# A transformer block with expert routing and row fetches, one core: the second half's attention is moved into the stage of the row fetches, its projections into the first half's tail

## The chip, the cores and the metric

The kernel runs on one core of one Trainium2 chip. The metric is the device time in microseconds of one execution. A core has the engines TensorE (PE, with its weight loads as PEld), VectorE (DVE), ScalarE (ACT), GpSimd (POOL) and SyncE (SP), each working through its own list of instructions in order, and 16 DMA engines. SP issues the weight loads, POOL issues indirect row fetches.

## The reference

All of it is float32, 256 tokens of width 1024. A first block (attention with a window, a convolution, a feed-forward of 16 experts) is followed by a second block, and only the second block matters here:

```
h = modulate(rmsnorm(x)); q, k, v, z, gl = split(h @ w_in)      # 7168 columns
q, k = rope(q), rope(k); k, v = concat(context, own)
for each of 8 heads: a = softmax(q1 k1) - lam * softmax(q2 k2); o = a @ v
y_attn = rmsnorm(o) @ w_branch_attn
y_sgu  = spatial_gating(gelu(z)) @ w_branch_sgu                  # per chunk of 128 tokens
x = x + gt1 * rmsnorm((sigmoid(ga) * y_attn + sigmoid(gs) * y_sgu) @ w_out)
# peer: 8 heads, each picks 16 of 16384 rows for each token
q = rmsnorm(modulate(rmsnorm(x)) @ w_query)
eidx, gate = two-stage top-16 of q @ sub_keys
out = sum_k gelu(h . u_tab[eidx_k]) * gate_k * v_tab[eidx_k]
return x + gt2 * rmsnorm(out)
```

## The kernel before

The 256 tokens are two halves of 128 (index `a`, 0 or 1). The second block, called the mixer here, follows one list of stages, `ORDER`, which `mixer_order` writes out; every engine walks the list and does its part of each stage, in order. The stages:

- `kq`, `vals`, `z`, `ga`, `gs`, `bs`, `ba`, `op` with `(n, a)` are "token groups": 16 matmuls (8 products, each as 2 instructions in the records) of one half against one 2 MB slab of weights (`tokens`, L379). `z` is the input of the spatial gating, `ga` and `gs` the gates, `bs` and `ba` the two branch products, `op` the output product. `zmix` (L689) mixes the tokens, `zturn` transposes its result.
- Attention has 16 units `ix` (half `a`, head `h`): `sc` (scores, L708), `exp` (DVE maxima L1199 to L1201, ACT exponentials L1629), `cmb` (DVE L1206 to L1213, with a scaled copy on ACT between, L1637), `trn` (transposes, L717), `av` (values, L728), `ao` (ACT).
- The tail of a half: `hn1`, `hn2`, `ht` (norm over the heads and transposes), `ba`, `bae`, `yt`, `op`, `ope`, `up1`, `up2`, `fn1`, `fn2`, `ft` (norms, residual, transposes L367). `gain1` and `gain2` spread a gain over the partitions (L737).
- The row stage: `take(a)` reserves four of the eight PSUM banks as accumulators, `qm(h, a)` (L771) and `qs` (L780) are the queries of one head (32 matmuls, slab `wq` of two heads), `back` turns the tokens back, `rt0` to `rt5` are the routing of one unit (DVE L1304 to L1379; the row numbers `ei` are ready after L1359). `row(ix, k)` is one fetch of 128 rows of 8 KB (1 MB, POOL L1739) and its dot product on DVE (L1368). `act` makes the weights on ACT (L1695, L1701), `v` multiplies two rows on PE (L813, 32 matmuls), which frees their two buffers. `leave(a)` (L825 on PE) folds the accumulators, applies a gain and a norm, and stores the half.

Order before. After `kq` and `vals`, ten steps handle units 0 to 7, each step followed by two token groups of a list `fill` of 20 (both halves of z, ga, gs, bs). Then comes the tail of half 0, and between its steps stand groups of the attention of units 8 to 15 (list `second`), two at a time. Then `take`, the queries of heads 0 to 3, nine more groups of `second`, `rt1` to `rt5` of unit 0, and the 256 rows. In the row stage one entry of the list `late` goes in at every third row: the queries of heads 4 to 7 of half 0, the tail of half 1, the queries of half 1. Routing stages stand at every row in unit 0 and at every odd row afterwards.

Weights: SP loads slabs into a ring of slots, [2, 3, 4, 5] in the mixer, [2, 3] once the row stage begins; a load waits until the slot's last user is done. A slab is loaded once for both halves in `z`, `ga`, `gs`, `bs`. Rows: eight buffers at first, four in the attention's scratch space (free after `av` of unit 15) and four in slots 4 and 5 (free after `op` of half 0), fixed in `row_places`; four more (slots 2 and 3) from the routing of unit 8 on.

Of the kernel before, what the change touches and what calls it, by code (L numbers as in the profile page):

```python
# [121 lines left out]
def build(nc, D, out):  # L122
    from contextlib import ExitStack
    ctx = ExitStack()
    with ctx:
# [71 lines left out]
        U, VV, SGT, GA = ar(o + 8192, 2, 1024), ar(o + 10240, 2, 1024), ar(o + 10240, 8, 256), ar(o + 12288, 2, 1024)  # L197
        RAW, RT, TMPG = ar(o + 14336, 2, 512), ar(o + 15360, 2, 512), ar(o + 14336, 2, 1024)
        PP, TT, AA, ATT = ar(o + 16384, 2, 2, 512), ar(o + 18432, 512), ar(o + 18944, 2, 512), ar(o + 19968, 2, 512)
        DM, OT, YT = ar(o + 20992, 16, 8), ar(o + 21120, 8, 128), ar(o + 22144, 8, 128)  # L200
        DG, G1, G2, OO, Y2 = ar(o + 10240, 8, 128), ar(o + 11264, 1024), ar(W0, 1024), XN, U
# [8 lines left out]
        RQ, DI, SG2 = ar(Q1 + 464, 2, 16), ar(Q1 + 496, 8, 2, 32), ar(o + 5120, 2, 16, 32)  # L210
# [14 lines left out]
        def mixer_order():  # L225
            todo = [("norm_turn", 0), ("kq", "k", 0, 0), ("norm_turn", 1), ("kq", "k", 0, 1), ("rope", "k", 0, 0)]
            held = ("rope", "k", 0, 1)
            for x, n in (("k", 1), ("q", 0), ("q", 1)):
                for a in range(2):
# [7 lines left out]
            def filler():  # L237
                while fill:
                    todo.append(fill.pop(0))
                    if todo[-1][0] in ("z", "ga", "gs", "bs"):  # L240
                        return

            for s in range(10):
# [6 lines left out]
                filler()  # L250
                if 1 <= s <= 8:
                    todo.append(("trn", s - 1))
                filler()
                if s >= 2:
                    todo += [("av", s - 2), ("ao", s - 2)]
            assert not fill
            second = []
            for s in range(8, 19):
                second.append([("sc", s)] * (s < 16) + [("trn", s - 2)] * (10 <= s < 18) + [("av", s - 3)] * (s >= 11))
                second.append([("cmb", s - 1)] * (9 <= s < 17) + [("exp", s)] * (s < 16) + [("ao", s - 3)] * (s >= 11))  # L260
# [34 lines left out]
            late = queries(2, 0) + queries(3, 0) + [h[0], h[1] + h[2]]  # L295
# [4 lines left out]
            for x in q[2:] + [[("back", 0)]] + queries(1, 0):  # L300
                todo += x
            queue(9)
            todo += [(f"rt{s}", 0) for s in range(1, 6)]
            routes = []
            for n in range(257):
# [9 lines left out]
                if n % 3 == 0 and late:  # L315
                    todo += late.pop(0)
# [6 lines left out]
            assert not late and not routes and not second  # L323
# [7 lines left out]
        ROWS = {}  # L331

        def row_places():
            def slots(i):
                return [NARENA + i * SLOT + x for x in range(0, 2 * SLOT, 2048)]

            bufs, n = [o + 16384, o + 18432, o + 2048, W0 + 2048] + slots(4), 0
            free = {k: ("mm", "av", 15) if i < 4 else ("used", "w_op", (i - 4) // 2, 0) for i, k in enumerate(bufs)}
            for stage, *x in ORDER:
                if (stage, *x) == ("rt0", 8):  # L340
                    new = slots(2)
                    free.update({k: ("used", "wq", 2 + i // 2, 1) for i, k in enumerate(new)})
                    bufs = bufs[:n] + new + bufs[n:]
                if stage == "row":
                    k = bufs[n]
                    n = (n + 1) % len(bufs)
                    ROWS[(*x,)] = k, free[k]
                    free[k] = ("mm", "row", x[0], x[1] // 2)

# [4 lines left out]
        def tensor(pe, w):  # L354
# [304 lines left out]
            def kq(x, n, a):  # L659
                tokens(("raw", x, n, a), ("w_in2", 2 + n if x == "k" else n), HT, a, h2m[a][:1], a == 1, h2m[a][1:])  # L660
# [10 lines left out]
            def vals(n, a):  # L671
                tokens(("vx", n, a), ("w_in2", 4 + n), HT, a, h2m[a], a == 1)

            def z(n, a):
                tokens(("z", n, a), ("w_in2", 6 + n), HT, a, h2m[a], a == 1)

            def ga(n, a):
                tokens(("gab", n, a), ("w_in2", 10 + n), HT, a, h2m[a], a == 1)

            def gs(n, a):  # L680
                tokens(("gsb", n, a), ("w_in2", 12 + n), HT, a, h2m[a], a == 1)
# [11 lines left out]
            def zturn():  # L693
                for a in range(2):
                    turn("copied", "sg", U[:, a, :], False, a, ("zmix", a, 1))

            def bs(n, a):
                tokens(("bs", n, a), ("w_bs", n), SGT, a, [("copied", "sg", 1, 1)], a == 1)
# [32 lines left out]
            def row_of(tag, *after):  # L731
                for q in range(2):
# [3 lines left out]
                    for j in range(4):  # L736
                        x = pe.matmul(PS[:, b, j * 128:(j + 1) * 128], ones, DG[:, 4 * q + j, :], start=True, stop=True)  # L737
# [5 lines left out]
            def ba(n, a):  # L743
                tokens(("ba", n, a), ("w_ba", n, a), OT, 0, [("scaled", "ot", a, 1)], True)
# [4 lines left out]
            def op(n, a):  # L749
                tokens(("y2sq", n, a), ("w_op", n, a), YT, 0, [("copied", "yt", a, 1)], True)  # L750
# [66 lines left out]
            def leave(a):  # L817
# [4 lines left out]
                for g in range(4):  # L822
                    w.wait_ge("part", a, g)
                    for m, (b, _) in enumerate(at):
                        x = pe.matmul(PS[32 * g:32 * g + 32, b, :], fold[:, m, :], PART[:, g, :], start=True, stop=True, skip_group_check=True)  # L825
                x.then_inc(*w.hit("mm", "leave", a, also=[("mm", "leave2", a)]))
# [11 lines left out]
        def vector(v, w):  # L838
# [376 lines left out]
            def row_of(tag, dst, col):  # L1215
                if tag == "g1":
                    w.wait_ge("mm", "bs", 1, 1)
# [6 lines left out]
                for j in range(8):  # L1224
                    i = v.tensor_scalar(DG[:, j, :], ident, col[:, j:j + 1], None, MULT)
# [19 lines left out]
            def heads_turn(a):  # L1245
                w.wait_step()
                w.wait_ge("gs", 1, 1)
                scaled("ot", OT, a, sub8, None)

            def bae(n, a):  # L1250
# [6 lines left out]
                w.wait_ge("bs", 1, 1)  # L1257
                v.tensor_tensor(y, y, g, ADD).then_inc(*w.hit("yy", n, a))

            def ope(n, a):  # L1260
                w.wait_ge("mm", "y2sq", n, a)
                w.wait_ge("row", "g1", 1)
                w.wait_ge("mm", "copied", "sg", 1, 1)
                v.tensor_tensor(Y2[:, a, n * 512:(n + 1) * 512], PS[:, banks.at("y2sq", n, a), :], G1[:, n * 512:(n + 1) * 512],
# [10 lines left out]
            def up2(a):  # L1275
                w.wait_ge("rstd", ("y2", a))
                w.wait_ge("y2", 1, a)
                v.scalar_tensor_tensor(X[:, a, :], Y2[:, a, :], ss5[:, a:a + 1], X[:, a, :], MULT, ADD).then_inc(*w.hit("x5", a))
# [91 lines left out]
            def rt5(ix):  # L1370
# [5 lines left out]
                w.wait_step()  # L1376
                if ix > 1:
# [4 lines left out]
            def leave(a):  # L1382
# [4 lines left out]
                for m in range(2):  # L1387
                    b = banks.at("leave", a, m)
                    w.wait_ge("sumsq", "out", a, m)
                    v.tensor_tensor(OUTS[a][:, m * 512:(m + 1) * 512], PS[:, b, :], G2[:, m * 512:(m + 1) * 512], MULT).then_inc(  # L1390
                        *w.hit("leave", a, m))
                w.step(v.tensor_tensor(SMX[:, a, 2:3], SMX[:, a, 2:3], SMX[:, a, 3:4], ADD))
                w.wait_step()
                rstd1(("out", a), SMX[:, a, 2:3], SMX[:, a, 2:3], 1024, 1e-6)
                rstd2(("out", a), SMX[:, a, 2:3])
                w.wait_ge("rstd", ("out", a))
                w.wait_ge("leave", a, 1)
                v.scalar_tensor_tensor(OUTS[a], OUTS[a], SMX[:, a, 2:3], X[:, a, :], MULT, ADD).then_inc(*w.hit("out", a))
# [12 lines left out]
        def scalar(act, w):  # L1411
# [197 lines left out]
            def zturn():  # L1609
                w.wait_ge("mm", "zmix", 1, 1)  # L1610
# [354 lines left out]
```

## Time and profile before

| what | value |
|---|---|
| median of 3 runs | 2239.13 us (2238.88 to 2240.02) |
| the profiled execution, its time | 2237.47 us |
| its span | 2235.7 us |
| PE busy | 1508.2 us (67%) |
| DVE busy | 753.6 us (34%) |
| ACT busy | 423.6 us (19%) |
| POOL busy | 297.8 us (13%) |
| read from HBM | 794.62 MB, 356 GB/s over the span |

The span is the profiled part of the execution; 1.8 us of its time lie around it. Busy shares are means over stages that differ: the first block runs up to about 1150 us, the mixer's dense part to about 1520 us, the row stage from there to the end. A clock of 1.00 is TensorE's full 2.4 GHz, 0.50 is 1.2 GHz.

### The profile page before, as it was taken

The numbers are of one execution on the slowest core, as the hardware profiler recorded it, in microseconds if no ns is written. First come the engines' busy times: TensorE is split into PE (matmuls) and PEld (weight loads), VectorE is DVE, ScalarE is ACT, GpSimd is POOL, SyncE is SP. The second block draws the span as 40 slices with busy tenths as digits, with TensorE's granted clock in tenths as the row PEclk, the third lists the DMA queues.
The fourth block names the chain that finished last, engine by engine and source line by source line (L and its number), as shares of the span: only waits on it lengthen the run. The fifth ranks groups of instructions, "written<-read, shape, count | busy, mean of one in ns | idle before, by whom it ended". The sixth has DMA issues, their size and how long they took to land.

```text
span 2235.7 us, 24542 instructions
## 1 busy us (share of the span) xinstructions
PE 1508.2 (67%) x10272; PEld 627.9 (28%) x10272; DVE 753.6 (34%) x1890; ACT 423.6 (19%) x983; POOL 297.8 (13%) x265
## 2 busy tenths in 40 slices
PE   8898756777766665665669999876655644444443
PEld 7555311332211111111124455454323421101010
DVE  5822101000000000000022141345657676776774
ACT  1321100000000000000011253243232332322221
POOL 0000000000000000000000000003333445444341
PEclk9988988988887878778779999987777865655555
DMA  9639999999999999999974332409999999999996
GB/s 382 236 152 423 427 426 427 426 427 427 428 426 427 427 427 427 427 427 426 428 319 170 135 139 84 188 18 367 420 419 377 420 416 415 412 420 420 419 419 270
DMA packets 74430, 797.46 MB, mean 357 GB/s; under 512 B 8304, under 2 KB 8432, under 8 KB 9424
## 3 DMA queue, kind: packets, MB, share of 16 engines
q1 hardware_dynamic: 37264, 527.25, 56.5%
q0 software_dynamic: 36864, 268.45, 29.1%
q8 instruction: 81, 1.33, 0.2%
q14 instruction: 29, 0.24, 0.0%
q10 hardware_dynamic: 192, 0.20, 0.0%
HBM read 794.62 MB, written 1.05 MB: 356 GB/s over the span
## 4 chain that ended last, share of the span: by engine, by line
DMA 46%; PE 32%; DVE 11%; POOL 4%; ACT 4%; issue 3%; another core or an unknown queue 0%; ACTq 0%; POOLq 0%; DVEq 0%
DMA AR<-in_w_down 18%; DMA AR<-in_w_up 15%; DMA AR<-in_peer_uv,AR 13%; PE PS L379 13%; POOL AR L1739 4%; DVE AR L1368 3%; PE PS L607 3%; PE PS L628 2%; PE PS L771 2%; PE PS L390 2%; PE PS L813 2%; PE PS L494 1%; DVE AR L890 1%; DVE AR L892 1%; PE PS L640 1%
## 5 line engine op out<-in xcount | busy, mean ns | idle before, releaser
L1739 POOL DMA_INDIRECT AR<-in_peer_uv,AR x256 | 296.0, 1156 | 1733.1 <-PE PS L728 1354.0
L813 PE MATMUL PS<-AR 32*32 32x512 f32 x4096 | 242.0, 921 | 328.5 <-ACT AR L1701 320.0
L607 PE MATMUL PS<-AR 128*32 128x512 f32 x2048 | 305.4, 734 | 181.0 <-DMA AR<-in_w_up 127.8
L1368 DVE CUSTOM_DVE_ANT_0 AR<-AR 128x1024 f32<-128x1024 f32 x256 | 309.7, 1222 | 166.3 <-DMA AR<-in_peer_uv,AR 153.1
L379 PE MATMUL PS<-AR 128*128 128x512 f32 x736 | 332.7, 607 | 2.4 <-DVE AR L865 1.9
L628 PE MATMUL PS<-AR 128*32 128x512 f32 x1024 | 173.3, 812 | 106.0 <-DMA AR<-in_w_down 99.2
L1064 DVE TENSOR_TENSOR AR<-AR,PS 128x512 f32<-128x512 f32 x16 | 11.0, 687 | 593.0 <-PE PS L607 593.0
L379 PEld LDWEIGHTS PS<-AR 128*128 128x128 f32 x736 | 140.2, 195 | 174.9 <-issue 174.6
L813 PEld LDWEIGHTS PS<-AR 32*32 32x32 f32 x4096 | 46.2, 127 | 479.9 <-ACT AR L1701 443.0
L607 PEld LDWEIGHTS PS<-AR 128*32 128x32 f32 x2048 | 63.9, 123 | 411.8 <-DMA AR<-in_w_up 204.3
L1078 DVE COPY AR<-PS 128x512 f32<-128x512 f32 x16 | 11.1, 691 | 284.7 <-PE PS L628 284.7
L628 PEld LDWEIGHTS PS<-AR 128*32 128x32 f32 x1024 | 33.5, 130 | 225.9 <-DMA AR<-in_w_down 149.8
L1522 ACT ACTIVATE AR<-PS 128x512 f32<-128x512 f32 x16 | 9.6, 597 | 398.4 <-PE PS L607 398.4
L390 PE MATMUL PS<-AR 128*128 128x256 f32 x384 | 83.4, 379 | 0.9 <-DVE AR L860 0.9
L640 PE MATMUL PS<-AR 128*128 128x512 f32 x128 | 68.4, 683 | 14.3 <-DVE AR L1078 13.5
L390 PEld LDWEIGHTS PS<-AR 128*128 128x128 f32 x384 | 72.9, 190 | 11.8 <-issue 2.0
L1695 ACT ACTIVATE AR<-AR 128x2 f32<-128x2 f32 x128 | 25.7, 201 | 249.0 <-DVE AR L1368 232.0
L771 PE MATMUL PS<-AR 128*128 128x128 f32 x512 | 70.7, 304 | 1.1 <-ACT PS L1651 1.1
L771 PEld LDWEIGHTS PS<-AR 128*128 128x128 f32 x512 | 68.2, 218 | 10.4 <-issue 10.4
L1701 ACT ACTIVATE AR<-AR 128x32 f32<-128x32 f32 x256 | 68.4, 314 | 9.2 <-ACT AR L1695 0.4
L1531 ACT COPY AR<-PS 128x512 f32<-128x512 f32 x16 | 9.4, 585 | 309.4 <-PE PS L617 309.4
L640 PEld LDWEIGHTS PS<-AR 128*128 128x128 f32 x128 | 26.7, 220 | 65.9 <-issue 65.9
(271 smaller groups left out, 1247.3 us busy)
## 6 DMA issues: line engine op xcount, KB each, us to landing
AR<-in_w_gate SPq DMA_DIRECT2D x64, 2048.0 KB, 26.1
AR<-in_w_up SPq DMA_DIRECT2D x64, 2048.0 KB, 24.7
AR<-in_w_down SPq DMA_DIRECT2D x64, 2048.0 KB, 26.0
AR<-in_w_in SPq DMA_DIRECT2D x23, 2048.0 KB, 8.7
AR<-in_w_ada SPq DMA_DIRECT2D x12, 2048.0 KB, 10.2
AR<-in_peer_w_query SPq DMA_DIRECT2D x8, 2048.0 KB
AR<-in_w_out SPq DMA_DIRECT2D x6, 2048.0 KB, 11.4
AR<-in_w_branch_attn SPq DMA_DIRECT2D x4, 2048.0 KB
```

Source lines behind the costliest of these rows:

```text
L379: i = pe.matmul(PS[:, b, :], src[:, j, a * 128:(a + 1) * 128], IN[key][:, j, :], start=(j == 0), stop=(j == 7))
L390: i = pe.matmul(PS[:, b, q * 256:(q + 1) * 256], IN[key][:, j, (e + q) * 128:(e + q + 1) * 128], src[:, j, :], start=(j == 0), stop=(j == 7))
L494: x = pe.matmul(PS[:, b, :], MT[:, 4 * q + j, a * 128:(a + 1) * 128], IN[key][:, j, n * 512:(n + 1) * 512], start=(j == 0), stop=(j == 3))
L607: x = pe.matmul(PS[32 * q:32 * q + 32, bk, :], XS[:, j, e * 32:(e + 1) * 32], IN[key][:, jj, q * 512:(q + 1) * 512], start=(j == 0), stop= ...
L628: x = pe.matmul(PS[32 * g:32 * g + 32, b, :], HDT[:, s, fq * 32:(fq + 1) * 32], IN[key][:, s, dc * 512:(dc + 1) * 512], start=(fq == 0 and ...
L640: x = pe.matmul(PS[:, y, :], GE[:, r, dc, a * 128:(a + 1) * 128], EO[:, r, :], start=(e == 0), stop=(e == 15), skip_group_check=True)
L771: x = pe.matmul(PS[:, b, q * 128:(q + 1) * 128], IN[key][:, j, (2 * r + q) * 128:(2 * r + q + 1) * 128], HT[:, j, a * 128:(a + 1) * 128], ...
L813: x = pe.matmul(PS[c:c + 32, ACC[a][g], :], DI[t, p, r, :], AR[t, off + 1024 + m * 512:off + 1536 + m * 512], start=(h == 0 and p == 0), s ...
L1368: v.tensor_tensor_reduce(rows, rows, HB[:, a, :], 1.0, 0.0, MULT, ADD, DOT[:, ix, k:k + 1]).then_inc(*w.hit("dot", ix, k))
L1695: w.step(act.activation(two, DOT[:, ix, 2 * p:2 * p + 2], ACT.Gelu))
L1701: i = act.activation(DI[:, p, r, :], SG2[:, ix % 2, 2 * p + r, :], ACT.Copy, scale=two[:, r:r + 1])
L1739: pool.indirect_dma_start(out=AR[:, off:off + 2048], out_offset=None, in_=D["peer_uv_2"], in_offset=bass.IndirectOffsetOnAxis(ap=EI[:, ix, ...
```

## The change

- The list of token groups is split. `first` (12 groups) keeps `z` 2 and 3 of both halves and everything of half 0; it stands between the steps of units 0 to 7, one group a step (two in steps 0 and 8). `then` (10 groups with `zmix` and `zturn` of half 1, that is `z`, `ga`, `gs`, `bs` of half 1) stands between the steps of half 0's tail, and its last, `bs(1, 1)`, after `rt5` of unit 0.
- The attention of units 8 to 15 (22 list entries) moves to the head of `late`, and `late` is taken at every second row in place of every third. Five empty entries stand before half 1's `ba`.
- All queries of half 0 stand before the first row.
- Slabs `z` 0 and 1, `ga`, `gs`, `bs` are loaded once for each half. The slot ring is [5, 2, 3, 4].
- The first eight row buffers are the two halves of each slot of the ring, free once `wq` 0, 1, 2, 3 of half 0 are used. After `ao` of unit 15 the four buffers of the scratch space come in, and slots 5 and 2 leave for weights; `w_ba` of half 1 waits for the last rows in them. Slots 5 and 2 come back at the routing of unit 8.
- `SGT`, `OT`, `YT`, `DG`, `Y2` become one tile for each half, `SG2` and `G1` move, and a few waits follow them.
- `leave` takes its two column halves apart: matmuls, squares, the last product and the store go half by half, and for half 1 ACT runs a square root on a spare value before the last rows are done.

```diff
-            fill = [("z", 2, 0), ("z", 2, 1), ("z", 3, 0), ("z", 3, 1), ("zn1",), ("z", 0, 0), ("zn2",), ("z", 0, 1), ("zn3",), ("z", 1, 0),
-                    ("z", 1, 1), ("zmix", 0), ("ga", 0, 0), ("zmix", 1), ("ga", 0, 1), ("ga", 1, 0), ("zturn",), ("ga", 1, 1)]
-            fill += [(f, n, a) for f in ("gs", "bs") for n in range(2) for a in range(2)]
+            first = [("z", 2, 0), ("z", 2, 1), ("z", 3, 0), ("z", 3, 1), ("zn1",), ("z", 0, 0), ("zn2",), ("z", 1, 0), ("zn3",), ("ga", 0, 0),
+                     ("zmix", 0), ("ga", 1, 0), ("zturn", 0), ("gs", 0, 0), ("gs", 1, 0), ("bs", 0, 0), ("bs", 1, 0)]
+            then = [("z", 0, 1), ("z", 1, 1), ("zmix", 1), ("ga", 0, 1), ("zturn", 1), ("ga", 1, 1), ("gs", 0, 1), ("gs", 1, 1), ("bs", 0, 1),
+                    ("bs", 1, 1)]
...
-            steps = h[:2], h[2:] + [[("gain1",)]], b[0], b[1], y, p[0], p[1], u[:2], u[2:4], u[4:]
-            for group in steps:
+            for group in (h[:2], h[2:] + [[("gain1",)]], b[0] + b[1], y, p[0] + p[1], u[:2], u[2:4]):
                 for x in group:
                     todo += x
-                queue(2)
+                filler(then)
+            todo += u[4]
...
-            late = queries(2, 0) + queries(3, 0) + [h[0], h[1] + h[2]]
+            late = []
+            for s in range(8, 19):
+                late.append([("sc", s)] * (s < 16) + [("trn", s - 2)] * (10 <= s < 18) + [("av", s - 3)] * (s >= 11))
+                late.append([("cmb", s - 1)] * (9 <= s < 17) + [("exp", s)] * (s < 16) + [("ao", s - 3)] * (s >= 11))
+            late += [h[0], h[1] + h[2]] + [[]] * 5
...
-            for x in q[2:] + [[("back", 0)]] + queries(1, 0):
+            for x in q[2:] + [[("back", 0)]]:
                 todo += x
-            queue(9)
             todo += [(f"rt{s}", 0) for s in range(1, 6)]
+            filler(then)
+            for x in queries(1, 0) + queries(2, 0) + queries(3, 0):
+                todo += x
...
-                if n % 3 == 0 and late:
+                if n % 2 == 0 and late:
                     todo += late.pop(0)
...
+        RING = [5, 2, 3, 4]
+            halves = [[NARENA + i * SLOT, NARENA + i * SLOT + 2048] for i in RING]
+            free = {k: ("used", "wq", i, 0) for i in range(4) for k in halves[i]}
+            bufs, gone = sum(halves, []), []
             for stage, *x in ORDER:
-                if (stage, *x) == ("rt0", 8):
-                    new = slots(2)
-                    free.update({k: ("used", "wq", 2 + i // 2, 1) for i, k in enumerate(new)})
-                    bufs = bufs[:n] + new + bufs[n:]
+                if (stage, *x) == ("ao", 15):
+                    new = [o + 2048, W0 + 2048, o + 16384, o + 18432]
+                    free.update({k: ("mm", "av", 15) for k in new})
+                    bufs, gone = bufs + new, halves[0] + halves[1]
+                elif (stage, *x) == ("rt0", 8):
+                    free.update({k: ("used", "wq", 2 + i, 1) for i in range(2) for k in halves[i]})
+                    bufs = bufs + halves[0] + halves[1]
...
+                if key[0] == "w_ba" and key[2] == 1:
+                    for half in (0, 2048):
+                        w.wait_ge(*LATEST[place[slot] + half])
...
             def leave(a):
+                if a:
+                    w.wait_ge("out", 0, 1)
+                    act.activation(SMX[:, 0, 3:4], ones[:, 0:1], ACT.Sqrt)
...
-                v.scalar_tensor_tensor(OUTS[a], OUTS[a], SMX[:, a, 2:3], X[:, a, :], MULT, ADD).then_inc(*w.hit("out", a))
+                for m in range(2):
+                    d = OUTS[a][:, m * 512:(m + 1) * 512]
+                    w.wait_ge("leave", a, m)
+                    v.scalar_tensor_tensor(d, d, SMX[:, a, 2:3], X[:, a, m * 512:(m + 1) * 512], MULT, ADD).then_inc(*w.hit("out", a, m))
```

## Rows read from the trace of the kernel before

**Rows 1.** The page's chain that ended last, shares by engine.
```profile
DMA 46%; PE 32%; DVE 11%; POOL 4%; ACT 4%; issue 3%; another core or an unknown queue 0%; ACTq 0%; POOLq 0%; DVEq 0%
```

**Rows 2.** Windows: stretch, length, busy of each engine, clock, DMA share, GB/s.
```profile
1157.00:1521.00 364.00, 336.55 (x1199) 182.93 (x1200) 108.10 (x275) 122.13 (x254) 0.95 (x1) 0.95 0.33 125
1521.00:1848.00 327.00, 195.06 (x2284) 101.19 (x2282) 220.03 (x577) 103.39 (x269) 132.97 (x113) 0.74 1.00 411
```

**Rows 3.** DMA queues from 1521 to 2219 us: packets, MB, share.
```profile
q0 software_dynamic: 36864, 268.45, 93.1%
q1 hardware_dynamic: 1368, 18.22, 6.2%
```

**Rows 4.** Timeline of DVE, ACT and SP at the span's end: start, length.
```profile
2162.65 1.22 DVE L1368 CUSTOM_DVE_ANT_0 AR<-AR 128x1024 f32<-128x1024 f32 x1
2163.80 1.22 DVE L1368 CUSTOM_DVE_ANT_0 AR<-AR 128x1024 f32<-128x1024 f32 x1
...
2216.55 1.23 DVE L1368 CUSTOM_DVE_ANT_0 AR<-AR 128x1024 f32<-128x1024 f32 x1 [1.26 <-DMA AR<-in_peer_uv,AR]
2219.03 1.22 DVE L1368 CUSTOM_DVE_ANT_0 AR<-AR 128x1024 f32<-128x1024 f32 x1 [1.24 <-DMA AR<-in_peer_uv,AR]
...
2229.57 1.28 ACT L1415 ACT_TABLE_LOAD   x1
...
2231.30 1.29 DVE L1398 SCALAR_TENSOR_TENSOR AR<-AR 128x1024 f32<-128x1024 f32 x1
```

**Rows 5.** Timeline of PE, steps of units 0 to 7 with token groups.
```profile
1253.88 1.14 PE L708 MATMUL PS<-AR 64*128 64x256 f32 x8
...
1276.91 0.60 PE L717 MATMUL PS<-PK,AR 128*128 128x128 f32 x4
1277.35 7.03 PE L379 MATMUL PS<-AR 128*128 128x512 f32 x16
...
1327.22 1.95 PE L689 MATMUL PS<-AR,PK 128*128 128x128 f32 x16
```

**Rows 6.** Timeline of PE, half 0's tail and queries.
```profile
1416.29 1.05 PE L728 MATMUL PS<-AR 128*128 128x128 f32 x8
...
1425.54 3.76 PE L737 MATMUL PS<-AR,PK 128*128 128x128 f32 x16 [3.33 <-DVE AR L1225]
...
1494.23 5.41 PE L771 MATMUL PS<-AR 128*128 128x128 f32 x32 [1.06 <-ACT PS L1651]
...
1507.57 3.74 PE L771 MATMUL PS<-AR 128*128 128x128 f32 x32
...
1512.75 3.82 PE L771 MATMUL PS<-AR 128*128 128x128 f32 x32
```

**Rows 7.** Timeline of DVE: one unit of attention, routing (first, last), first row.
```profile
1431.48 0.75 DVE L1213 SCALAR_TENSOR_TENSOR AR<-AR 128x512 f32<-128x512 f32 x1 [0.79 <-ACT AR L1637]
1432.14 0.68 DVE L1199 TENSOR_REDUCE AR<-PS 128x1 f32<-128x512 f32 x1
...
1502.10 0.61 DVE L1304 TENSOR_SCALAR AR<-PS,AR 128x128 f32<-128x128 f32 x2
...
1512.06 0.17 DVE L1359 CAST AR<-AR 128x16 uint32<-128x16 f32 x1
...
1527.71 1.23 DVE L1368 CUSTOM_DVE_ANT_0 AR<-AR 128x1024 f32<-128x1024 f32 x1 [4.96 <-DMA AR<-in_peer_uv,AR]
```

**Rows 8.** Timeline of POOL: the first row fetch.
```profile
1520.05 1.08 POOL L1739 DMA_INDIRECT AR<-in_peer_uv,AR  x1 [1353.99 <-PE PS L728]
```

**Rows 9.** Line L1368 (dots of rows) from 1521 to 1848 us.
```profile
L1368 DVE CUSTOM_DVE_ANT_0 AR<-AR x109: 1202/1222/1265, 1527.7 to 1845.7; 128x1024 f32<-128x1024 f32 x109
```

**Rows 10.** Timeline of PE, two token groups in the row stage.
```profile
1602.45 9.29 PE L379 MATMUL PS<-AR 128*128 128x512 f32 x16
...
1612.74 7.13 PE L379 MATMUL PS<-AR 128*128 128x512 f32 x16
```

**Rows 11.** Windows of 10 us in the row stage, the emptiest (columns as rows 2).
```profile
1690.00:1700.00 10.00, 4.96 (x76) 2.13 (x74) 7.12 (x23) 5.29 (x13) 2.24 (x2) 0.78 0.59 220
```

More of the change, by code:

```diff
@@ L249, in mixer_order @@
                     todo.append(("exp", s))
-                filler()
+                filler(first)
                 if 1 <= s <= 8:
                     todo.append(("trn", s - 1))
-                filler()
+                if s in (0, 8):
+                    filler(first)
                 if s >= 2:
                     todo += [("av", s - 2), ("ao", s - 2)]
[L256 to L260, printed above, removed]
+            assert not first
             def tail(a):
@@ L691, in zmix, with zturn @@
                     x.then_inc(*w.hit("mm", "zmix", a, q))
-            def zturn():
-                for a in range(2):
-                    turn("copied", "sg", U[:, a, :], False, a, ("zmix", a, 1))
+            def zturn(a):
+                turn("copied", "sg", U[:, a, :], False, a, ("zmix", a, 1))
             def bs(n, a):
-                tokens(("bs", n, a), ("w_bs", n), SGT, a, [("copied", "sg", 1, 1)], a == 1)
+                tokens(("bs", n, a), ("w_bs", n, a), SGT[a], 0, [("copied", "sg", a, 1)], True)
             def att_scores(ix):
@@ L1607, in zn1, with zturn @@
                     act.activation(Y[:, a, :], VV[:, a, :], ACT.Square, accum_out=smv[:, 4 + a:5 + a]).then_inc(*w.hit("sumsq", "zv", a))
-            def zturn():
-                w.wait_ge("mm", "zmix", 1, 1)
-                for a in range(2):
-                    copied("sg", SGT[:, :, a * 128:(a + 1) * 128], a)
+            def zturn(a):
+                w.wait_ge("mm", "zmix", a, 1)
+                copied("sg", SGT[a], a)
             def ga(n, a):
@@ L1823, in sync @@
                     load(NS + 3, ("rows",), D["rows"].partition_broadcast(128), 2, 1024)
-                elif stage == "bs" and x[1] == 0:
-                    square(("w_bs", x[0]), "w_branch_sgu_2", x[0])
-                elif stage == "gain1":
-                    turn[0] = 0
+                elif stage == "bs" and x != [1, 1]:
+                    square(("w_bs", *x), "w_branch_sgu_2", x[0])
                 elif stage == "take" and x[0] == 0:
-                    turn[0], ids[0] = 0, [2, 3]
+                    square(("w_bs", 1, 1), "w_branch_sgu_2", 1)
+                    assert turn[0] % 4 == 0
+                elif (stage, *x) == ("hn1", 1):
+                    turn[0], ids[0] = 0, RING[:2]
                 elif stage == "ba":
@@ L1837, in sync @@
                     a = x[0]
-                    w.wait_ge("out", a)
-                    sp.dma_start(out[a * 128:(a + 1) * 128, :], OUTS[a]).then_inc(*w.hit("stored", a, by=16))
-            w.wait_ge("stored", 1)
+                    for m in range(2):
+                        f = slice(m * 512, (m + 1) * 512)
+                        w.wait_ge("out", a, m)
+                        sp.dma_start(out[a * 128:(a + 1) * 128, f], OUTS[a][:, f]).then_inc(*w.hit("stored", a, m, by=16))
+            w.wait_ge("stored", 1, 1)
         for dry in (True, False):
```

102 lines of the change are left out of this document (54 added, 48 removed).

## The prediction

> **What bounds the kernel now.** I read the chain that ended last first: it lies on DMA for 46% and on PE for 32% [rows 1]. Windows tell where. From 1157 to 1521 us PE is busy for 336.6 of 364 us while DMA is busy for a third; from 1521 us on DMA is busy throughout and PE for 60% [rows 2]. So there are two stages: a dense one that PE's sum sets, and a row stage that the DMA traffic sets, from the first fetch on. Work that goes from the first under the second is free as long as it keeps the fetches fed. In the row stage 268.45 MB are rows and 18.22 MB the other traffic [rows 3]; where nothing disturbs it a row comes every 2.49 us (2216.55 to 2219.03) [rows 4]. A DVE dot costs 1.15 us when two follow each other [rows 4], so DVE has 1.34 us to spare for each row. The first dot starts at 1527.7 us and the 109th at 1845.7 us [rows 9]; 108 rows of 2.49 us and eight slabs of 5 us (2.1 MB at 420 GB/s) are 309 us, so 9 us of DMA time are lost in this half, some 4 of them near 1695 us, in half 1's tail [rows 11].
>
> **Before the rows.** The dense stage is costed as a sum on PE. A token group takes 7.0 us (7.03 less the overlap with its neighbour), `zmix` 1.9 for a half, `zturn` 0.9 for a half (8 matmuls where `zmix` has 16 in 1.95) [rows 5]. A unit of attention costs PE 1.06 + 0.44 + 0.98 = 2.5 us (L708, L717, L728, start to start) [rows 5, 6]. The first scores start at 1253.9 us. The ten steps keep 12 groups (83.5 us), 8 units (19.8), one `zmix` and one `zturn` (2.8): 106 us. Each step is now 9.5 us instead of 16.4; a unit's work on DVE is 3.5 us (cmb 0.75, maxima 2 x 0.68, small ones, 0.8 of waiting for ACT's copy) [rows 7], so it fits, and I add 2 us for stalls (0 to 6). The last `av` then ends at 1362 us; before it does at 1417.3 [rows 6].
>
> The tail of half 0 now has whole token groups between its steps. On PE: ten groups before `ft` (z 2, ba 2, ga 2, op 2, gs 2: 70), one more (bs, 7), `zmix`, `zturn`, `yt` (3.7), `ht` with the stall and `gain1` (1.0 + 3.3 + 3.8 [rows 6]) = 89 us, then 4.6 us from the start of `ft` to the first query (transposes, four DVE products of 0.7). The norms of the tail hide under the groups: each is a pass or two over a half and a root, 1.3 us each [rows 4], and a group lasts 7. Queries start at 1455.4 us (before 1494.2). From that start to `ei` it was 17.9 us (1512.1) [rows 6, 7], of which 1.7 us are a slow clock (5.41 against 3.74 us for one query) [rows 6]. The first row can be issued at 1472 us, 48 us earlier than at 1520.05 [rows 8].
>
> But it isn't worth 48 us. The fetches of rows 2 and 3, 4 and 5, 6 and 7 wait for queries 3, 5 and 7, and `v` of rows 0 and 1, which frees the next buffers, stands in PE's list behind all of them. PE: query 0 and rt0 5.7 us, query 1 and `back` 6.0, `bs(1, 1)` 7.0, six queries at 5.2 (1507.57 to 1512.75 [rows 6]) 31.2; PE reaches the rows at 1505.3 us, and queries 3, 5, 7 end at 1483, 1493.4 and 1503.8. ACT's and DVE's lists have the same barrier: the root in `rt0` of unit 1 stands behind the last query. From there DVE sets the pace: dots 1 to 7 (8.1), routing of unit 1 (11.5: 10.1 from 1502.1 to 1512.2 [rows 7], and an estimate of 1.4 for rt0 and rt5), two units' maxima and one `cmb` (5.2), 25.3 us in all, to 1530.6. With `act` 0.7, `v` 2.0 and the issue 0.3, rows 14 and 15 are issued at 1533.7; a fetch lands 5.4 us after its issue (1520.05 to 1527.7, less 2.2 us for a rest of a slab that is still under way: 18.22 MB less eight slabs and the store of 0.5 is 0.9 MB) [rows 3, 7, 8]. Row 14 lands at 1539.1; at 2.49 us a row that is as if row 0 had landed at 1504.2, against 1527.7: **-23.5 us**.
>
> **Under the rows.** Eight units over 44 rows (109.6 us of DMA). DVE's sum: 44 dots 50.6, three routings 34.5, eight units 28 = 113 us. It falls behind by 4 us in 16 rows and is some 11 us late at row 44. A ring of eight buffers (19.9 us) forgives 9 us, so I take 3 us of loss; the bounds are 0 (waits overlap) and 10 (each step waits 1 us more). It doesn't come back, since DMA is the bound afterwards. The tail of half 1 goes at two rows a step (5.0 us, or 7.5 where a slab is loaded too) instead of three: four token groups of 7.1 to 9.3 us [rows 10] and eight `v` of 1.1 to 2.0 us stand against 16 rows (40 us) with some four slabs (20 us), 54 us of PE against 60 of DMA. But in the three steps of norms DVE waits 3 us for ACT's root each time, and each step is now 2.5 us shorter, 7.5 us together; before, such a place cost 4 us [rows 11]. I take 5 us of loss; the bounds are 0 and 12. The queries of half 1 fit (17 us of PE against 15 and two slabs in a cycle of three steps). DMA's bytes hardly change: slabs that are now loaded twice are loaded in the dense stage, where DMA is busy for a third [rows 2], 5 us of traffic in a group of 7 us, four slots ahead; the 0.9 MB fall away, already counted.
>
> The clock: in the dense stage 0.95 is granted, in the row stage 0.74 [rows 2], and a token group takes 9.29 us after a lull and 7.13 right behind another [rows 10]. The Trainium skill says in "TensorE: Matmul & The Clock Gate", section "What's actually happening", that the array runs at half rate by default and activity releases it; this trace agrees (0.95 against 0.74). By that rule, units moved to where PE is sparse cost 40 instead of 20 us of PE and the four groups 37 instead of 28, which PE's slack takes up.
>
> **The end.** `leave` of half 1: the 1.28 us table load before the root goes off the chain, and the last product of 1.29 us is split [rows 4]. About 0.4 us of the load are covered by DVE's work; the last piece ends 0.9 us earlier, its store is smaller: **-1.3 us** (bounds -0.5 and -2.5).
>
> **Sum.** -23.5 + 3 + 5 - 1.3 = -16.8 us, on the profiled execution's own 2237.5 us: 2220.7. That execution is 1.7 us below the median of the runs, so 2222 us.
>
> **Rivals.**
> - *The rows stay fed from the queries on.* If DVE gets ahead in the first eight rows (waits of ACT and PE overlap more than I count) and the tail loses nothing new, row 6 issued at 1503.8 lands at 1509.2, as if row 0 had landed at 1494.3: -33.4 - 1.3 = -35, 2204 us. For it: DVE is busy for 220 of 327 us there [rows 2]. Against: 25 us of DVE work stand in its first eight rows.
> - *The whole 48 us come.* Needs rows 2 to 7 not to wait for the queries; the buffers exclude it. About 2190, nearly no chance.
> - *The other side: the steps at every second row.* In the first 104 rows DVE has 120 us of dots, 75 of routing, 28 of attention and some 39 of tail, gains and norms, 262 us, against 299 us of DMA (104 x 2.49 and eight slabs). With the ring's 9 us, what DVE waits for PE and ACT in these 52 steps beyond 46 us (0.9 us a step) is lost. I have put 8 us of loss; at 1.4 us of waiting a step 25 us are lost and the gain is nothing, at 1.7 us a step it ends at 2255 us. For it: DVE waits 0.8 us for ACT in each unit [rows 7] and PE holds `v` back for 7 to 9 us at a token group. Against: DVE idles for a third of this half now [rows 2].
> - *Weights late in the dense stage.* Ten more slabs; against it the ring is four deep, 28 us of work. Each late slab would cost up to 5 us; it takes three to be seen.
>
> **How the numbers follow.** Under 0.2% (4.5 us) this kernel's measurement can't tell a change from none. My forecast with its own bounds (2212 to 2234) has a chance of 0.5, fed from the start (below 2212) 0.28, a result within 4.5 us of before 0.1 and slower 0.12, nearly all of both by the steps at every second row. The range leaves out a tenth on each side: 2200 to 2240. Faster 0.78, same 0.10, slower 0.12.
>
> **What would show it.** The profile after should have the last `av` of unit 7 near 1362 us, the first query near 1455, the first fetch near 1472, rows 2, 4 and 6 issued near 1483, 1493 and 1504, then dense fetches from about 1534. DMA's share should be 1.00 from there with short holes in the attention's last rows and in half 1's tail, and the last dot starts near 2203. I am wrong if holes of more than 25 us together stand in the first 104 rows, if PE waits for slabs before the rows, or if DVE isn't what paces the first eight rows.

## The result, and the profile after

The changed kernel takes 2251.92 us (median of 4 runs, 2251.43 to 2254.99) against 2239.01 us for the kernel before beside it: ratio 1.0061, interval 1.0043 to 1.0078. It is slower; the forecast was 17 us faster. The profiled execution took 2251.69 us with a span of 2249.9, 14.2 us longer than before.

The page's slices already show two different halves of the answer: DMA works much more in the dense stage, and has holes where it used to be full. Windows of the kernel after, columns as in [rows 2]:

```profile
1154.00:1465.00 311.00, 298.80 (x944) 152.12 (x945) 87.30 (x220) 94.37 (x178) 0.00 (x0) 0.97 0.53 197
1465.00:1540.00 75.00, 45.07 (x446) 31.42 (x444) 35.89 (x97) 30.41 (x66) 20.85 (x18) 0.77 0.70 258
1540.00:1860.00 320.00, 187.03 (x2044) 99.32 (x2028) 201.21 (x536) 121.20 (x293) 107.27 (x93) 0.71 0.89 355
```

The dense stage is over 56 us earlier than in [rows 2]. In exchange the stage behind it, which ran at 1.00 of DMA before (the second window of [rows 2]), runs at 0.89, and in the mean of its 320 us no engine is full: DVE 63%, PE 58%, ACT 38%.

The dense part went as the forecast says. Timeline of PE after (L737 is `av`, L746 `gain1`, L780 the first query), to be laid beside [rows 6]:

```profile
1355.97 1.05 PE L737 MATMUL PS<-AR 128*128 128x128 f32 x8
...
1367.34 2.59 PE L746 MATMUL PS<-AR,PK 128*128 128x128 f32 x16 [2.58 <-DVE AR L1235]
...
1446.80 5.44 PE L780 MATMUL PS<-AR 128*128 128x128 f32 x32 [2.64 <-DVE AR L874]
```

and of POOL, which answers to [rows 8]:

```profile
1465.17 1.08 POOL L1758 DMA_INDIRECT AR<-in_peer_uv,AR  x1 [1302.00 <-DVE AR L1370]
...
1476.36 0.94 POOL L1758 DMA_INDIRECT AR<-in_peer_uv,AR  x1 [8.86 <-PE PS L780]
...
1486.87 0.94 POOL L1758 DMA_INDIRECT AR<-in_peer_uv,AR  x1 [8.34 <-PE PS L780]
...
1497.38 0.94 POOL L1758 DMA_INDIRECT AR<-in_peer_uv,AR  x1 [8.33 <-PE PS L780]
...
1512.43 1.87 POOL L1758 DMA_INDIRECT AR<-in_peer_uv,AR  x1 [5.30 <-PE PS L822]
...
1528.77 0.94 POOL L1758 DMA_INDIRECT AR<-in_peer_uv,AR  x1 [4.90 <-PE PS L822]
```

The first fetch is issued at 1465 us (before 1520), rows 2, 4 and 6 wait for queries 3, 5 and 7 (L780), and row 14 goes out at 1528.8 where 1533.7 was forecast. The gain is there at that point. The next table tells where it goes: the start of row n's dot product, in us, read from DVE's timeline of each kernel (one profiled execution of each; executions of one kernel differ by some us, so small differences of such stretches say little).

| row | before | after | after minus before |
|---|---|---|---|
| 0 | 1527.7 | 1471.0 | -56.7 |
| 8 | 1553.3 | 1524.4 | -28.9 |
| 48 | 1681.7 | 1646.6 | -35.1 |
| 72 | 1751.5 | 1742.2 | -9.3 |
| 112 | 1855.7 | 1872.8 | +17.1 |
| 255 | 2219.0 | 2234.9 | +15.9 |

Rows 8 to 112 need, by the prices of the prediction, 104 x 2.49 us and eight slabs of 5 us, 299 us of DMA. Before took 302.4, after takes 348.4: 3 us lost before, 49 after. The kernel before has issued six of its eight slabs by row 48 (at 1540.6 to 1649.7 us), the changed one none (its first at 1655.8), so -35.1 at row 48 hides that it is behind already: its 122.2 us for 40 rows are 22.6 more than their 99.6 of DMA, and the next 64 rows with eight slabs (199.4 us) lose 27 more. From row 112 on both run at the pace of DMA.

What such a hole is made of, in an attention entry. Timeline of the kernel after (L822 is `v`, L717 `sc`, L726 `trn`, L1659 ACT's copy of the transposes, L1698 the routing's exponential, L1711 and L1717 the weights of two rows):

```profile
1578.82 2.02 PE L822 MATMUL PS<-AR 32*32 32x512 f32 x32 [6.62 <-ACT AR L1717]
...
1580.78 2.08 PE L717 MATMUL PS<-AR 64*128 64x256 f32 x8
...
1582.78 1.09 PE L726 MATMUL PS<-PK,AR 128*128 128x128 f32 x4
...
1583.91 0.59 ACT L1659 COPY AR<-PS 128x512 f32<-128x512 f32 x1 [5.14 <-PE PS L726]
...
1584.52 1.28 ACT L1698 ACT_TABLE_LOAD   x1
...
1585.81 0.31 ACT L1698 ACTIVATE AR<-AR 128x16 f32<-128x16 f32 x1
...
1586.23 1.28 ACT L1711 ACT_TABLE_LOAD   x1
...
1587.53 0.20 ACT L1711 ACTIVATE AR<-AR 128x2 f32<-128x2 f32 x1
...
1587.76 0.53 ACT L1717 ACTIVATE AR<-AR 128x32 f32<-128x32 f32 x2
...
1588.35 2.02 PE L822 MATMUL PS<-AR 32*32 32x512 f32 x32 [3.58 <-ACT AR L1717]
```

One `v` follows another after 9.5 us, where two rows of DMA last 5.0. It is one of the three longest such rounds of rows 8 to 48, where a pair of rows takes 6.1 us in the mean. The 9.5 us are a chain with one link after another: `v` 2.0, `sc` 2.0, `trn` 1.1, ACT's copy 0.6, a table load 1.3, the exponential 0.4, another load 1.3, the weights 0.8. The dots of those two rows had ended at 1581.9; their weights wait in ACT's list until 1587.5, behind a copy that waits for PE, and PE had this `trn` behind the previous `v`. In the tail of half 1 the same list waits for DVE:

```profile
1739.94 2.02 PE L822 MATMUL PS<-AR 32*32 32x512 f32 x32 [5.68 <-ACT AR L1717]
...
1742.21 1.22 DVE L1379 CUSTOM_DVE_ANT_0 AR<-AR 128x1024 f32<-128x1024 f32 x1
...
1747.97 1.22 DVE L1379 CUSTOM_DVE_ANT_0 AR<-AR 128x1024 f32<-128x1024 f32 x1
...
1752.15 0.15 DVE L1371 TENSOR_SCALAR AR<-AR 128x1 f32<-128x1 f32 x1
...
1752.33 0.31 ACT L1698 ACTIVATE AR<-AR 128x16 f32<-128x16 f32 x1 [11.14 <-DVE AR L1371]
1752.75 1.28 ACT L1711 ACT_TABLE_LOAD   x1
...
1754.04 0.20 ACT L1711 ACTIVATE AR<-AR 128x2 f32<-128x2 f32 x1
...
1754.86 2.02 PE L822 MATMUL PS<-AR 32*32 32x512 f32 x32 [8.74 <-ACT AR L1717]
...
1757.80 0.95 POOL L1758 DMA_INDIRECT AR<-in_peer_uv,AR  x1 [12.32 <-PE PS L822]
```

The two dots are done at 1749.1. Their weights stand behind the routing's exponential, which waits until DVE has finished that unit's routing at 1752.2. ACT idles for 11 us, and POOL gets its next free buffer after 12.3 us. DMA's share is 0.53 in the window from 1750 to 1760 us. The order is not all of this hole: the dots themselves end only at 1749.1, since DVE does work of the tail between them and is busy for 8.5 and 9.7 of the 10 us from 1740 and from 1750 on. The order costs what lies between 1749.1 and 1754.0, when the weights start: 4.9 us. So DVE, at 63% in the mean, is full in just this place.

### The profile page after: what moved, and what is told of

Read it like the earlier page. It is cut to its first block, busy times and chain, and to the rows that moved or that the text cites. A ratio compares the mean times of both kernels' runs of the same rounds, so it can differ in the third digit from the quotient of the medians.

```text
span 2249.9 us, 24580 instructions
## 1 busy us (share of the span) xinstructions
PE 1503.2 (67%) x10272; PEld 625.4 (28%) x10272; DVE 751.3 (33%) x1892; ACT 445.1 (20%) x1000; POOL 295.2 (13%) x265
## 4 chain that ended last, share of the span: by engine, by line
DMA 43%; PE 34%; DVE 12%; ACT 6%; POOL 3%; issue 2%; ACTq 0%; POOLq 0%; DVEq 0%
DMA AR<-in_w_down 18%; DMA AR<-in_w_up 15%; PE PS L389 14%; DMA AR<-in_peer_uv,AR 10%; PE PS L780 3%; POOL AR L1758 3%; DVE AR L1379 3%; PE PS L822 3%; PE PS L617 2%; PE PS L638 2%; PE PS L400 2%; DVE AR L899 1%; PE PS L504 1%; DVE AR L901 1%; ACT L1711 1%
## 5 line engine op out<-in xcount | busy, mean ns | idle before, releaser
L822 PE MATMUL PS<-AR 32*32 32x512 f32 x4096 | 233.5, 945 | 363.4 <-ACT AR L1717 363.4
L1379 DVE CUSTOM_DVE_ANT_0 AR<-AR 128x1024 f32<-128x1024 f32 x256 | 308.2, 1221 | 126.7 <-DMA AR<-in_peer_uv,AR 126.7
L389 PEld LDWEIGHTS PS<-AR 128*128 128x128 f32 x736 | 140.4, 194 | 175.0 <-issue 174.3
L822 PEld LDWEIGHTS PS<-AR 32*32 32x32 f32 x4096 | 41.8, 127 | 508.9 <-ACT AR L1717 498.0
L400 PEld LDWEIGHTS PS<-AR 128*128 128x128 f32 x384 | 72.9, 190 | 12.0 <-issue 2.2
L1711 ACT ACTIVATE AR<-AR 128x2 f32<-128x2 f32 x128 | 25.8, 202 | 235.3 <-DVE AR L1379 234.6
L780 PE MATMUL PS<-AR 128*128 128x128 f32 x512 | 70.0, 302 | 2.6 <-DVE AR L874 2.6
L780 PEld LDWEIGHTS PS<-AR 128*128 128x128 f32 x512 | 67.5, 216 | 10.8 <-issue 10.8
L1717 ACT ACTIVATE AR<-AR 128x32 f32<-128x32 f32 x256 | 68.3, 314 | 9.3 <-ACT AR L1711 0.7
L1711 ACT ACT_TABLE_LOAD x41 | 52.6, 1283 | 0.7
```

Source lines behind the costliest of these rows:

```text
L389: i = pe.matmul(PS[:, b, :], src[:, j, a * 128:(a + 1) * 128], IN[key][:, j, :], start=(j == 0), stop=(j == 7))
L400: i = pe.matmul(PS[:, b, q * 256:(q + 1) * 256], IN[key][:, j, (e + q) * 128:(e + q + 1) * 128], src[:, j, :], start=(j == 0), stop=(j == 7))
L780: x = pe.matmul(PS[:, b, q * 128:(q + 1) * 128], IN[key][:, j, (2 * r + q) * 128:(2 * r + q + 1) * 128], HT[:, j, a * 128:(a + 1) * 128], ...
L822: x = pe.matmul(PS[c:c + 32, ACC[a][g], :], DI[t, p, r, :], AR[t, off + 1024 + m * 512:off + 1536 + m * 512], start=(h == 0 and p == 0), s ...
L1379: v.tensor_tensor_reduce(rows, rows, HB[:, a, :], 1.0, 0.0, MULT, ADD, DOT[:, ix, k:k + 1]).then_inc(*w.hit("dot", ix, k))
L1711: w.step(act.activation(two, DOT[:, ix, 2 * p:2 * p + 2], ACT.Gelu))
```

## The experiments

Theory "queue": the weights of two rows, which free their buffers through `v`, stand in ACT's list behind work that waits for PE or DVE, and that loop takes longer than the fetches of two rows. Against it: "sum" (DVE or PE has too much work at any spacing), "ring" (the eight buffers in slots that weights share), "tables" (ACT's table loads are the long part). Each kernel below was timed beside the kernel before on its own chip, so ratios are compared; 1.0061 is the changed kernel's. The intervals stand in brackets.

**Spacing.** In each kernel one condition is changed; the first two also have fewer empty entries.

```diff
 # att3_rest2
-            late += [h[0], h[1] + h[2]] + [[]] * 5
+            late += [h[0], h[1] + h[2]] + [[]] * 2
-                if n % 2 == 0 and late:
+                if (n % 3 == 0 if n < 66 else n % 2 == 0) and late:
 # att2_rest3
-            late += [h[0], h[1] + h[2]] + [[]] * 5
+            late += [h[0], h[1] + h[2]] + [[]] * 0
-                if n % 2 == 0 and late:
+                if (n % 2 == 0 if n < 44 else (n - 44) % 3 == 0) and late:
 # before_step2, in the kernel before
-                if n % 3 == 0 and late:
+                if n % 2 == 0 and late:
```

> Changed kernel with one edit: the 22 attention entries at every third row, the rest still at every second (two of the five empty entries kept so that it fits). Theory 'step' (each entry makes DVE, ACT and PE wait for one another inside two rows' time; some 28 us of fetch time are lost over rows 0 to 48 and some 27 over the tail and queries of half 1): the first loss falls to about 10 us, the second stays, so about 2235 us. Theory 'sum' (DVE has too much work whatever the spacing): no change, 2250 us or more. Theory 'ring' (eight buffers among slots that weights share are the cause): no change.

2232.56 us, ratio 0.9974 (0.9964 to 0.9984). The attention at every third row takes back 19 us. Rows 8 to 48 now take 109.9 us instead of 122.2, rows 48 to 112 213.9 instead of 226.2. Over rows 8 to 112 together that is 323.8 us instead of 348.4, while DVE is busy for 219 us of them (217 in the changed kernel), so "sum" falls. 5 us of this are given back in rows 112 to 128 (56.6 instead of 51.5), where the last two queries of half 1 now stand. The split between the two stretches says less, since 13 attention entries stand in rows 8 to 47 at this spacing and 18 in the changed kernel. The second loss shrank although six attention entries moved into it, which was not expected.

> Changed kernel with one edit: attention entries at every second row as now, the tail and queries of half 1 at every third, no empty entries. Theory 'step': the loss over rows 48 to 112 falls from 27 us to the 9 us that the kernel before shows in all this half, about 2234 us; the attention's loss stays. Theory 'sum': the same 2250. Theory 'ring': about 2250, and without the empty entries PE waits for slabs, 5 us more.

2258.1 us, ratio 1.0096 (1.0073 to 1.0118): a miss for all the theories as they stood. Two things cancel. PE's timeline shows long waits before its two `ba` groups, since the empty entries that gave their slabs time are gone (the first wait has no releaser in the profile; its slab was issued at 1657.9, 11.6 us ahead of the group):

```profile
1669.52 9.38 PE L389 MATMUL PS<-AR 128*128 128x512 f32 x16 [11.75 <-issue]
...
1689.00 9.88 PE L389 MATMUL PS<-AR 128*128 128x512 f32 x16 [9.04 <-DMA AR<-in_w_branch_attn]
```

Rows 48 to 72 take 107.7 us (95.6 in the changed kernel), rows 72 to 112 take 115.5 (130.6). So rows 72 to 112 gained 15 us, and the missing empty entries took 12. Not all of the 15 is won: at this spacing the last two queries of half 1 stand behind row 110, and rows 112 to 128 take 4 us more (55.5 for 51.5).

> The kernel before with one edit: its late entries at every second row instead of every third (nothing else of the change). Theory 'step': the denser steps alone cost it some 10 to 20 us, 2249 to 2259 us. Theories 'sum' and 'ring': work and buffers are the same, so 2239 us, within 4 us.

2250.09 us, ratio 1.0053 (1.0035 to 1.0071). With none of the change's moves, every second row alone costs the kernel before 11 us: rows 8 to 112 take 315.4 us instead of 302.4. The denser steps are a cost of their own.

**The attention back ahead of the rows.**

```diff
-            for x in queries(1, 0) + queries(2, 0) + queries(3, 0):
+            for x in units[:4]:
                 todo += x
+            for i, x in enumerate(queries(1, 0) + queries(2, 0) + queries(3, 0)):
+                todo += x
+                for y in units[4 + 2 * i:min(22, 4 + 2 * i + 2)]:
+                    todo += y
```

(`units` are the 22 attention entries, taken out of `late`.)

> Changed kernel with its attention of half 1 put back before the rows, between the queries of heads 2 to 7, where DVE idles for some 30 us; the rest as in the changed kernel (every second row, five empty entries). Eight units cost PE some 20 us there, so rows from the eighth on come about 20 us later; the 28 us of loss over rows 0 to 48 should go under theories 'step' and 'sum' alike: 2240 to 2246 us. Under 'ring' the loss stays and it is 20 us worse, 2270 us.

2261.32 us, ratio 1.0109 (1.009 to 1.0128): worse, and not for the ring. Row 8's dot starts at 1570.9 us, 46 us later than in the changed kernel where 20 were expected, since PE waits for ACT's exponentials between the queries. One of these places, on PE (L784 are the queries there):

```profile
1482.58 5.47 PE L784 MATMUL PS<-AR 128*128 128x128 f32 x32 [3.33 <-ACT AR L1649]
```

From row 8 to 112 it takes 310.1 us, 11 more than DMA needs, at the same two-row steps. That does not settle "ring", because the buffers are not the same: the exchange of buffers hangs on `ao` of unit 15, which now stands ahead of row 0, so that from row 8 on four of the eight lie in the scratch space, as in the kernel before. Against "ring" stand before_step2, which loses its 13 us without the changed ring, and the next edit, which leaves the ring as it is. Units of attention without token groups between them cost 46 us ahead of the rows and, if the whole difference is theirs, some 38 (49 less 11) under them.

**ACT's order.** In the row stage ACT's part of the transposes, the queries and the routing's exponential goes behind the next weights; nothing else moves. This is the edit to ACT's walk through the list:

```diff
             for stage, *x in ORDER:
-                if stage in mine:
+                rows = rows or stage == "row"
+                if rows and stage in ("trn", "qm", "rt4"):
+                    late.append((stage, x))
+                elif stage in mine:
                     mine[stage](*x)
+                if stage == "act":
+                    for name, y in late:
+                        mine[name](*y)
+                    late = []
```

> Changed kernel with ACT's own order edited in the row stage: its part of the transposes, of the queries and of the routing's exponential goes behind the next weights of rows instead of ahead of them. Theory 'queue' (the weights of two rows, which free their buffers through v, stand in ACT's list behind work that waits for PE or DVE; the loop dot, entry, weights, v, fetch then takes longer than two rows of DMA): at least 20 of the 45 us of extra loss go, about 2225 us. Theory 'engines too full' (DVE's or PE's sum): 2250 us, no change. Theory 'step' without the queue behind it (PE and DVE waits alone): 2245 to 2250 us.

2224.12 us, ratio 0.9935 (0.9919 to 0.9952): 28 us of the changed kernel's time gone by an order of instructions alone, with the same ring, spacing and work; between 1500 and 1860 us ACT loads a table 48 times instead of 50, so it is not fewer table loads. Rows 8 to 112 take 311.4 us instead of 348.4 (row 8 itself starts 7 us later, at 1531.2). Rows 48 to 112 take 197.9, their DMA time. Rows 8 to 48 take 113.5 instead of 122.2: 14 of the 22.6 us lost there stay. Windows of this kernel:

```profile
1465.00:1540.00 75.00, 46.17 (x423) 32.53 (x421) 34.37 (x100) 26.78 (x59) 17.61 (x17) 0.82 0.64 237
1540.00:1830.00 290.00, 181.24 (x2092) 95.83 (x2092) 203.81 (x539) 121.69 (x297) 110.97 (x96) 0.76 0.98 399
```

DVE's 204 us fit in 290 us (before the edit 201 in 320), and DMA is at 0.98. The list of waits from 1500 to 1860 us (engine and line, who for, us in all, times, longest) says which wait became which. After:

```profile
POOL AR L1758 <- PE PS L822: 221.7, 43, 12.3
...
DVE AR L856 <- ACT AR L1430: 64.1, 10, 28.1
ACT AR L1711 <- DVE AR L1379: 50.5, 10, 13.4
ACT AR L1686 <- PE PS L780: 46.5, 8, 8.0
ACT AR L1659 <- PE PS L726: 34.6, 8, 5.2
ACT AR L1698 <- DVE AR L1371: 29.8, 4, 11.1
```

and in act_first:

```profile
POOL AR L1768 <- PE PS L822: 182.7, 49, 12.6
...
ACT AR L1711 <- DVE AR L1379: 115.1, 34, 14.0
...
DVE AR L856 <- ACT AR L1430: 38.4, 11, 28.1
ACT AR L1686 <- PE PS L780: 27.1, 9, 5.2
```

ACT's weights now wait for their own dot products (L1379), 34 times instead of 10, and its waits for PE's transposes (L1659) are 10.6 us in all and those of the routing's exponential for DVE (L1698) 4.1. DVE gains too: its waits for a square root on ACT (L856) fall from 36.0 to 10.3 us, when the 28.1 us behind the barrier of queries are left out.

The three parts one by one, each with only its own stage in the tuple `("trn", "qm", "rt4")`:

> Changed kernel; of the edit of ACT's order only the routing's exponential is moved behind the next weights. The whole edit brought 28 us. ACT stood up to 11 us before this exponential once for each of seven units of half 0: if that is the main part, 13 to 18 us of the 28 come, 2237 us; if the queue behind PE (transposes, queries) is, under 8 us, 2246 us.

2241.51 us, ratio 1.0017 (1.0007 to 1.0027).

> Changed kernel; only ACT's part of the queries is moved behind the next weights. ACT waited 46 us for the eight queries of half 1: if these waits sit in the loop, 8 to 12 us of the 28 come, 2242 us; if DMA was fed anyway there, nothing, 2252 us.

2239.35 us, ratio 1.0002 (0.9992 to 1.0011).

> Changed kernel; only ACT's copy of the transposed weights of attention is moved behind the next weights. ACT waited 35 us for the eight transposes: if these waits sit in the loop, 5 to 10 us of the 28 come, 2244 us; if DVE's sum bounds the attention's rows, nothing, 2252 us.

2240.74 us, ratio 1.0009 (0.9998 to 1.0019).

Against 1.0061 these are 10, 13 and 12 us, 35 together where all three at once give 28: three of the same kind, none of them the main one. The queries' part works mostly in rows 88 to 112 (62.6 us instead of 74.6), the transposes' part mostly in rows 8 to 48 (113.4 instead of 122.2).

> The kernel before with the same edit of ACT's order. Its row stage has DMA at 1.00 nearly everywhere, so under any theory little is to be had: 'queue' gives 2234 to 2239 us (part of the 9 us lost in half 0), the others 2239 us.

2232.88 us, ratio 0.9964 (0.9952 to 0.9976), 8 us less, somewhat more than expected. The queue is in the kernel before as well; at three rows a step it costs it little.

> Changed kernel in which the rows' weights leave out the Gelu (a plain copy of the dot product in its place), so that ACT needs no table load before them. Theory 'tables' (two loads of 1.28 us for each unit, root or exponential, lengthen the loop): of 45 us of extra loss 15 to 25 go, about 2230 us. Theory 'queue' with waits for PE and DVE as the long part: 5 to 10 us go, about 2243 us.

2232.56 us, ratio 0.9964 (0.9952 to 0.9976), 22 us below the changed kernel, as "tables" had it. This kernel leaves out the Gelu, and between 1500 and 1860 us it loads a table 15 times instead of 50. So "tables" stands beside "queue" and does not fall. The two don't contradict each other: the loads are links of the same chain, and the chain gets shorter by any of its links. No kernel has both edits, so what they share is not known.

> Attention entries at every third row (2232.6 us alone) with the edit of ACT's order. Theory 'queue': the losses left there (10 us over rows 8 to 48, 15 over 48 to 112) halve, about 2220 us. If spacing and order cure the same thing in full, 2230 us; 'engines too full' 2233 us.

2211.96 us, ratio 0.9884 (0.9862 to 0.9906), the fastest kernel here: 26 us below the one before. Rows 8 to 112 take 308.3 us, 9 above DMA's time, and rows 8 to 48 of them 105.7, 6 above theirs.

**The barrier of queries.** Two conditions and a list: the queries of heads 6 and 7 leave the front and come first in `late`.

```diff
-            for x in queries(1, 0) + queries(2, 0) + queries(3, 0):
+            for x in queries(1, 0) + queries(2, 0):
-            late = []
+            late = queries(3, 0)
-                if (n % 3 == 0 if n < 66 else n % 2 == 0) and late:
+                if (n % 2 == 0 if n < 6 or n >= 72 else n % 3 == 0) and late:
```

> The kernel with attention at every third row and the edit of ACT's order (2212 us), in which the queries of heads 6 and 7 also go behind the first rows (entries at rows 0, 2 and 4). If the barrier of queries before the rows is what leaves DMA at 0.6 to 0.8 from 1480 to 1540 us, PE reaches the rows 10 us earlier and 5 to 9 us come: 2205 us. If DVE's routing in the first eight rows is, 2212 us.

2213.24 us, ratio 0.9891 (0.9873 to 0.9908): no gain over 0.9884. Row 8 starts at 1515.1 us instead of 1524.0, as expected of the barrier, and row 112 at 1818.6 instead of 1832.3, but at row 128 the two are level (1883.1 and 1884.5). The last 16 rows of the half take 64.5 us (52.2 in att3_act_first). The trace shows two reasons. The last `wq` slab of half 1 is issued at 1825.5 us, behind row 112 here and ahead of it there (1816.5), which only moves 5 us. The rest is a hole, with DMA's share at 0.39 from 1850 to 1860 us. The fetch of row 124 goes to slot 2, which is free only when slab `wq` 3 is used up, and the query that ends its use stands behind row 122 here and behind row 116 there. So POOL stands before this fetch for 10.5 us (4.0 in att3_act_first), with all later fetches behind it. This, too, is an item that waits at the head of an engine's list, this time POOL's.

## Why the prediction was wrong

- **The start of the rows** (-23.5 us) was right in its mechanism and 5 us too careful, by its own steps: 1356.8 us for the end of the last `av` (forecast 1362), 1446.8 for the first query (1455), 1465 for the first fetch (1472), 1528.8 for row 14 (1533.7). Half of the difference was there when the first scores started, at 1251.2 instead of 1253.9 us; most of the rest are the 2 us of stalls that I had added and that did not come. DVE did pace the first eight rows: it waited until 1500.4 us for the root behind the last query (forecast 1505.3) and ended dot 7 at 1524.5, 24.1 us later. The recorded parts of that stretch (8.1, 11.5 and 5.2) add up to 24.8 us, not 25.3. Row 8 is 28.9 us earlier than before.
- **Attention under the rows (+3 us, bounds 0 to 10) is the step that failed first.** It measured 22.6 us over rows 8 to 48. The step compared DVE's sum with DMA's time and gave the ring 9 us of forgiveness. (By its own sum, 113 us against 109.6, DVE would be 3.5 us late at row 44 and not 11.) But DVE's sum didn't set the pace: DVE was busy for 86.1 of the 122.2 us, less than the 99.6 that DMA needs. What was missing is the round from one `v` to the next, through three engines' lists, which a sum per engine can't see because none of the three is full in the mean. ACT alone waited 34.6 us there for PE's transposes (L1659), in eight places. How much of the 22.6 us is ACT's order is shown in part: act_first takes 9 away with the same work in the same rows. The other 14 stay at this spacing; with the attention at every third row as well (att3_act_first) it is 6. Which waits of PE and DVE make them up is open.
- **The tail at every second row (+5 us, bounds 0 to 12)** measured 27 us over rows 48 to 112, where the kernel before, with two slabs left, loses some 5. The step looked for DVE's waits for the roots of the norms, 3 us each; in the trace they are 0.7, 1.1 and 1.4 us. The long waits of this stretch were ACT's, for PE's queries (46.5 us in eight places) and for DVE's routing (17.9 in two), and behind ACT those of DVE for the root of a routing's start (9.2 us before 1776.9 and 10.4 before 1836.1). act_first takes all of these 27 us away, and before_step2 shows that the denser steps cost 13 us over rows 8 to 112 without the rest of the change.
- **The end** (-1.3 us): from the start of the last dot to the end of the span it was 16.7 us [rows 4] and is 15.0, so -1.7. The table load before the root is off the chain, at 2236.99, beside the last `v`:

```profile
2234.87 1.23 DVE L1379 CUSTOM_DVE_ANT_0 AR<-AR 128x1024 f32<-128x1024 f32 x1 [1.26 <-DMA AR<-in_peer_uv,AR]
...
2236.99 1.28 ACT L1723 ACT_TABLE_LOAD   x1
...
2245.99 1.41 DVE L1413 SCALAR_TENSOR_TENSOR AR<-AR 128x512 f32<-128x512 f32 x2
```

- **The rivals.** "The steps at every second row" came true, and its point was about right: it needed 41 us of loss for 2255 us, and 49 were lost behind a better start. It got a chance of 0.12 because the waiting was priced by single waits of DVE (0.8 us in a unit [rows 7]). The rival itself named the sign, a token group that holds `v` back for 7 to 9 us [rows 10], but the sum counted such a group as a load on PE only. Its 262 us of work for DVE were too many (217 busy over rows 8 to 112), so the loss came with more room than the rival gave it. The prediction's own sign of being wrong, holes of more than 25 us in these rows, came true. "Weights late in the dense stage" did not happen: none of PE's waits from 1154 to 1465 us is for a slab.

The sum with the measured terms: -28.9 at row 8, +46 for the 49.4 us against 3.4 that rows 8 to 112 lost, -1 behind them and -1.7 at the end are +14, the +14.2 of the span.

## What to carry to other kernels

Before work is moved under a stream of transfers, write out the round that frees a buffer, with everything that stands ahead of each of its links in each engine's list, and compare that with the time of the transfers; a mean of two thirds busy says nothing about it, and an engine at 63% in the mean can be full in the very hole. In a list that several engines walk together, the instruction that frees a buffer belongs ahead of work that waits for another engine. Here 28 us came from that order alone, and spacing and order together made out of a change that was 13 us slower one that is 26 us faster.

## What the runs showed of the hardware

- ACT's table loads did not wait for the instruction they serve: the load for the routing's exponential ran at 1739.90 us in the changed kernel and its activation, which waited for DVE, at 1752.33. An activation can start 1.29 us after its load has started (1585.81, and 1587.53 after 1586.23). The Trainium skill ("ScalarE: Activation LUTs", section "What ACT_TABLE_LOAD costs") gives 1283 ns for the load, which the trace shows, and some 1.38 us of drain on top, 2.66 us for a switch; this trace shows no such drain (ACT's copy of 0.59 us starts at 1583.91 and the load at 1584.52), and the measurement decides: a switch costs 1.3 us here. With Exp, Gelu and Sqrt taking turns the rows' weights alone load a table 25 times between 1500 and 1860 us.
- The same attention scores (8 matmuls of 256 columns) took 1.14 us at 1567.99 us in the changed kernel, with a granted clock of 1.00 and PE at work just before, and 2.08 us at 1580.78, with a granted clock of 0.50 (1.2 GHz) from 1578.8 to 1582.8, after PE had been idle for 6.6 us ahead of the `v` in front of them. Over the row stage from 1540 to 1860 us the clock is 0.71 in the mean. A `v` took 1.15 us at 1566.90 and 2.02 us at 1578.82. So the holes make the PE links of such a round longer. What that adds to the loss is not shown.
